# Prepared weights in groups of 1024 columns, four words apart, in a two-model transformer kernel

## The reference, cut to what matters

```python
for l in range(2):                                     # first block
    h = rmsnorm(x, norm_mix[l]); proj = h @ w_in[l]    # q, k, v, u, ug, ga, gb
    merged = sigmoid(ga) * attention(q, k, v) + sigmoid(gb) * (conv(u, ug) @ w_conv_out[l])
    x = x + merged @ w_out[l]
    g, up = split(rmsnorm(x, norm_ffn[l]) @ w_gate_up[l])
    x = x + (silu(g) * up) @ w_down[l]                 # w_down: 2816 x 1024
proj = rmsnorm(x, g_pre_mix_2) @ w_in_2                # second block
y_ret = retention(q, k, v, g) @ w_ret_o_2
y_sgu = (gelu(u) * spatial(layernorm(gelu(sv)))) @ w_sgu_o_2
x = x + rmsnorm((sigmoid(a_ret) * y_ret + sigmoid(a_sgu) * y_sgu) @ w_out_2, g_post_mix_2)
x = x + rmsnorm(conv_gated_mlp(rmsnorm(x, g_pre_ffn_2), w_up_2, w_down_2), g_post_ffn_2)
```

## Time and profile before

| what | value |
|---|---|
| median of the 2 runs | 2197.49 us (2197.23 to 2197.76) |
| span of the profiled execution | 2195.6 us |
| TensorE busy (10,528 matmuls) | 2182.7 us, 99% |
| weight loads busy | 1813.8 us, 83% |
| VectorE busy | 1378.5 us, 63% |
| ScalarE busy | 965.5 us, 44% |
| GpSimd busy | 74.7 us, 3% |
| DMA | 208.39 MB, 95 GB/s, 27% of the 16 engines' time |

### The profile page before, as it was taken

How to read it: one execution, slowest core, us unless ns; L and a number is a source line. 1 busy time by engine, 2 the same in 40 slices (tenths; PEclk the granted TensorE clock), 3 DMA queues, 4 the chain that set the end, 5 groups by cost and what they waited for, 6 DMA issues and landing times.

```text
span 2195.6 us, 28930 instructions
## 1 busy us (share of the span) xinstructions
PE 2182.7 (99%) x10528; PEld 1813.8 (83%) x10528; DVE 1378.5 (63%) x1978; ACT 965.5 (44%) x1392; POOL 74.7 (3%) x103
## 2 busy tenths in 40 slices
PE   9999999999999999999999999999999999999998
PEld 6878888888888878888888888888888899888887
DVE  7999954444345999954444334654776568888723
ACT  5678544443223588544443223331554344333412
POOL 0000020000010000020000010000000000000000
PEclk9999999999999999999999999999999999999999
DMA  5221222222223211222222224223222231222222
GB/s 182 75 78 65 96 96 96 96 96 84 93 93 123 90 62 64 94 96 100 99 99 92 80 92 156 97 77 131 84 91 87 96 135 39 100 101 97 94 96 77
DMA packets 35397, 208.39 MB, mean 95 GB/s; under 512 B 4512, under 2 KB 5024, under 8 KB 14816
## 3 DMA queue, kind: packets, MB, share of 16 engines
q1 hardware_dynamic: 35296, 207.07, 27.0%
HBM read 201.15 MB, written 2.10 MB: 93 GB/s over the span
## 4 chain that ended last, share of the span: by engine, by line
PE 94%; ACT 3%; DVE 2%; issue 1%; DMA 0%; SPq 0%; DVEq 0%
PE mm L1794 25%; PE mm L1796 25%; PE mm L1795 25%; PE sp L1794 4%; PE sp L1795 4%; PE sp L1796 4%; PE sp L1896 1%; PE ob L1924 1%; DVE conv_y L1171 1%; ACT probs L584 1%; DVE probs L1201 1%; ACT probs L592 1%; PE sp L1911 0%; DMA x<-in_x_dram 0%; PE ob L1796 0%
## 5 line engine op out<-in xcount | busy, mean ns | idle before, releaser
L1794 PE MATMUL mm<-in_hi,w_hi 128*128 128x512 f32 (+1 forms) x1696 | 663.8, 391 | 3.8 <-DVE in_lo L1104 2.1
L1796 PE MATMUL mm<-in_hi,w_lo 128*128 128x512 f32 (+1 forms) x1696 | 657.0, 387 | 0.0
L1795 PE MATMUL mm<-in_lo,w_hi 128*128 128x512 f32 (+1 forms) x1696 | 657.0, 387 | 0.0
L525 ACT ACTIVATE w_hi<-w_raw 128x2048 fp32r<-128x2048 f32 (+3 forms) x193 | 346.2, 1794 | 674.8 <-PE mm L1796 557.9
L1070 DVE TENSOR_TENSOR w_lo<-w_raw,w_hi 128x2048 fp32r<-128x2048 f32 (+3 forms) x193 | 422.3, 2189 | 239.5 <-ACT w_hi L525 239.0
L1794 PEld LDWEIGHTS mm<-in_hi,w_hi 128*128 128x128 f32 x1696 | 318.5, 188 | 75.1 <-DVE in_lo L1104 6.0
L1796 PEld LDWEIGHTS mm<-in_hi,w_lo 128*128 128x128 f32 x1696 | 318.4, 188 | 65.8
L1795 PEld LDWEIGHTS mm<-in_lo,w_hi 128*128 128x128 f32 x1696 | 318.6, 188 | 64.1 <-issue 1.0
L1171 DVE SCALAR_TENSOR_TENSOR conv_y<-conv_in,parl,conv_y 128x512 f32<-128x512 f32 x240 | 170.0, 747 | 1.7
L1081 DVE TENSOR_TENSOR tB<-mm,rstd 128x512 f32<-128x512 f32 x54 | 37.3, 691 | 172.8 <-PE mm L1796 172.8
L1794 PE MATMUL mm<-act_hi,w_hi 128*128 128x512 f32 x352 | 136.9, 389 | 0.0
(11 more groups left out here) (429 smaller groups left out, 3257.0 us busy)
## 6 DMA issues: line engine op xcount, KB each, us to landing
w_raw<-in_w_dram SPq DMA_DIRECT2D x160, 1024.0 KB, 4.8
w_raw<-in_w_dram SPq DMA_DIRECT2D x32, 704.0 KB, 3.9
w_raw<-in_w_dram SPq DMA_DIRECT2D x5, 512.0 KB, 4.7
out_dram<-z_rows SPq DMA_DIRECT2D x8, 256.0 KB, 2.1
rope<-in_rope_dram SPq DMA_DIRECT2D x3, 512.0 KB, 3.6
x<-in_x_dram SPq DMA_DIRECT2D x4, 256.0 KB, 4.9
x<-in_x_dram SPq DMA_DIRECT2D x2, 512.0 KB, 7.9
sq<-ssum SPq DMA_DIRECT2D x32, 32.0 KB, 1.8
```

The lines of the kernel that those rows point to most:

```text
L525: e.activation(whi[:, slot, 0:cols], raw[:, slot, 0:cols], ACT.Copy).then_inc(s_whi, whi_out.up())
L1794: MM(out, ah, bh, start=first, stop=False, **kw)
L1795: MM(out, ah, bl, start=False, stop=False, **kw)
L1796: return MM(out, al, bh, start=False, stop=last, **kw)
```

## The change

The slots of w_hi and w_lo become two groups of 1028 columns, of which 1024 are used: the tensors are [128, 2, 2, 1028] in place of [128, 2, 2048]. From the tensor's start, the tiles of slot 0 group 0 begin at multiples of 512 bytes as before, those of slot 0 group 1, slot 1 group 0 and slot 1 group 1 at 16, 32 and 48 bytes past one. Each tensor is 64 bytes longer. The unused tensor to_512_bytes goes. w_raw and the loads stay as they are.

Helpers turn a column range into a place. A range of more than 1024 columns always becomes both groups whole, 2048 columns; so down's preparation of 1408 columns, on ScalarE and on VectorE, now works on 2048, of which the last 640 hold what an earlier chunk left.

```diff
+GROUP = CH // 2 + 4
...
-        whi = sb("w_hi", [P, 2, CH], F32R)
-        wlo = sb("w_lo", [P, 2, CH], F32R)
+        whi = sb("w_hi", [P, 2, 2, GROUP], F32R)
+        wlo = sb("w_lo", [P, 2, 2, GROUP], F32R)
...
-        sb("to_512_bytes", [P, 92])
...
+        def w_cols(t, slot, a, b):
+
+            h = CH // 2
+            if b - a > h:
+                return t[:, slot, 0:2, 0:h]
+            return t[:, slot, a // h, a % h:a % h + b - a]
+
+        def w_tile(t, slot, k):
+
+            return t[:, slot, k // KT, k % KT * P:k % KT * P + P]
+
+        def raw_cols(slot, a, b):
+
+            if b - a > CH // 2:
+                return raw[:, slot, :].rearrange("p (k c) -> p k c", k=2)
+            return raw[:, slot, a:b]
...
-                e.activation(whi[:, slot, 0:cols], raw[:, slot, 0:cols], ACT.Copy).then_inc(s_whi, whi_out.up())
+                e.activation(w_cols(whi, slot, 0, cols), raw_cols(slot, 0, cols), ACT.Copy).then_inc(s_whi, whi_out.up())
...
-                TT(wlo[:, slot, first:cols], raw[:, slot, first:cols], r32(whi[:, slot, first:cols]),
+                TT(w_cols(wlo, slot, first, cols), raw_cols(slot, first, cols), r32(w_cols(whi, slot, first, cols)),
                    ALU.subtract).then_inc(s_w, w_out.up())
...
-                    a = slice((at + j) * P, (at + j + 1) * P)
-                    ins = mm3(four[bank], whi[:, slot, a], wlo[:, slot, a], hi_[:, k, :], lo_[:, k, :],
+                    ins = mm3(four[bank], w_tile(whi, slot, at + j), w_tile(wlo, slot, at + j), hi_[:, k, :], lo_[:, k, :],
                               first and j == 0, last and j == len(ks) - 1)
...
-                    ws = slice(j * D + d * T, j * D + d * T + T)
+                    ws = (c % 2, j * D + d * T, j * D + d * T + T)
...
-                    ins = mm3(rows[b][d], acth[:, k, ts], actl[:, k, ts], whi[:, c % 2, ws], wlo[:, c % 2, ws],
+                    ins = mm3(rows[b][d], acth[:, k, ts], actl[:, k, ts], w_cols(whi, *ws), w_cols(wlo, *ws),
                               k == 0, k == FT - 1)
```

More of the change, by code:

```diff
@@ L533, in prep_part @@
             def prep_part(cs):
-                e.activation(whi[:, 0, cs], raw[:, 0, cs], ACT.Copy).then_inc(s_whi, whi_out.up())
+                e.activation(w_cols(whi, 0, cs.start, cs.stop), raw_cols(0, cs.start, cs.stop), ACT.Copy).then_inc(s_whi, whi_out.up())
             def prep_rest():
@@ L1115, in prep_and_sum @@
                 for cs in (slice(0, CH // 2), slice(CH // 2, CH)):
-                    TT(wlo[:, 1, cs], raw[:, 1, cs], r32(whi[:, 1, cs]), ALU.subtract).then_inc(s_w, w_out.up())
+                    TT(w_cols(wlo, 1, cs.start, cs.stop), raw_cols(1, cs.start, cs.stop),
+                       r32(w_cols(whi, 1, cs.start, cs.stop)), ALU.subtract).then_inc(s_w, w_out.up())
                     if cs.start == 0:
@@ L1136, in _ @@
             first_lo((2,))
-            more = slice(CH // 4, CH // 2)
             e.wait_ge(s_whi, whi_in.next())
-            TT(wlo[:, 0, more], raw[:, 0, more], r32(whi[:, 0, more]), ALU.subtract).then_inc(s_do, own.up())
+            TT(w_cols(wlo, 0, CH // 4, CH // 2), raw_cols(0, CH // 4, CH // 2), r32(w_cols(whi, 0, CH // 4, CH // 2)),
+               ALU.subtract).then_inc(s_do, own.up())
             first_lo((3,))
@@ L2011, in token_major @@
                         e.wait_ge(ready.sem, ready.next())
-                    ws = slice(256 * k, 256 * k + 256)
-                    ins = mm3(mm[bank][:, 0:256], xh[:, k, ts], xl[:, k, ts], whi[:, slot, ws], wlo[:, slot, ws],
+                    ws = (slot, 256 * k, 256 * k + 256)
+                    ins = mm3(mm[bank][:, 0:256], xh[:, k, ts], xl[:, k, ts], w_cols(whi, *ws), w_cols(wlo, *ws),
                               k == 0, k == KT - 1)
@@ L2025, in wide @@
                         e.wait_ge(ready.sem, ready.next())
-                    ws = slice(T * j, T * j + T)
-                    ins = mm3(four[wide_banks[b]], xh[:, k, ts], xl[:, k, ts], whi[:, slot, ws], wlo[:, slot, ws],
+                    ws = (slot, T * j, T * j + T)
+                    ins = mm3(four[wide_banks[b]], xh[:, k, ts], xl[:, k, ts], w_cols(whi, *ws), w_cols(wlo, *ws),
                               k == 0, k == KT - 1)
@@ L2122, in half_product @@
                         e.wait_ge(ready.sem, ready.next())
-                    a = slice(at + k * P, at + (k + 1) * P)
-                    ins = mm3(out, wh[:, a], wl[:, a], xh[:, k, hs], xl[:, k, hs], k == 0, k == KT - 1)
+                    a = slice(k * P, (k + 1) * P)
+                    ins = mm3(out, wh[:, at, a], wl[:, at, a], xh[:, k, hs], xl[:, k, hs], k == 0, k == KT - 1)
                 return ins
@@ L2136, in out_half @@
             def out_half(m, hs, ks=range(KT), ready=None):
-                return half_product(four[m % 4][:, 0:TH], wo[:, m // 2, 0, :], wo[:, m // 2, 1, :],
-                                    CH // 2 * (m % 2), hs, ready, ks)
+                wh, wl = (wo[:, m // 2, i, :].rearrange("p (k c) -> p k c", k=2) for i in range(2))
+                return half_product(four[m % 4][:, 0:TH], wh, wl, m % 2, hs, ready, ks)
             def up_half(j, hs, ks=range(KT), ready=None):
-                return half_product(four[j][:, hs], whi[:, j // 2, :], wlo[:, j // 2, :],
-                                    CH // 2 * (j % 2), hs, ready, ks)
+                return half_product(four[j][:, hs], whi[:, j // 2, :, :], wlo[:, j // 2, :, :],
+                                    j % 2, hs, ready, ks)
             e.wait_ge(s_w, w_in.next())
@@ L2192, in _ @@
                         e.wait_ge(s_mmf, taken.next())
-                        half_product(bank, whi[:, c, :], wlo[:, c, :], CH // 2 * d,
+                        half_product(bank, whi[:, c, :, :], wlo[:, c, :, :], d,
                                      slice(0, T)).then_inc(s_mm, tiles.up())
```

## The result

| kernel | median us (lowest to highest) | runs | span of the profiled execution |
|---|---|---|---|
| before | 2197.49 (2197.23 to 2197.76) | 2 | 2195.6 |
| changed | 2235.17 (2234.96 to 2235.38) | 2 | 2233.1 |

The changed kernel takes 1.0172 times the time of before, with a 95% interval of 1.0156 to 1.0189: +37.7 us, where +17.6 was forecast. The time moved the way that was forecast but a little over twice as far, to where rival C had put it (2231 to 2240).

A forecast was written before the change was run, and what follows sets the result against it. TensorE's pace was taken to bound the kernel. Terms of 9.3 and 8.3 us, the others 0, gave +17.6 us: 2213 on the profiled span, 2215 us by the median; own range 2198 to 2231, stated range 2180 to 2264.

The forecast's parts named there:

- rival C: All products: groups change faster than the rhythm settles, or settling needs phase 0; +33 to +43 us, 2231 to 2240; chance 0.14.
- What bounds the kernel: Whole kernel: TensorE busy 2182.7 of 2195.6 us at full clock; only its pace or a new wait can change the time.
- Part 1: Stationary weight tiles: each of 344 changes of group disturbs the rhythm for 27 ns, +9.3 us; bounds 0 to 18 us.
- Part 2: Weights as streamed operand (wide, token_major, rows_product): 828 shifted matmuls at 10 ns, +8.3 us; bounds 0 and 11.
- Part 3: Pad gone, weight tensors 64 bytes longer, so w_lo, x and in_hi move: taken at 0, bound 10 ns a product.
- rival D: Toll: every product with a shifted operand pays 10 ns wherever that operand sits; +66 us, 2263 us; chance 0.13.
- Part 4: Preparation, down's 1,408 columns rounded up to 2,048 on ScalarE and VectorE: covered, taken at 0; +4 us if slack is overdrawn.
- the 15.0 forecast: Down loop: sign that the prediction is right, its 66 matmuls taking 15.0 us.
- A (relief): Shifted products escape a 13.3 ns collision of weight load and stream: -88 us, 2110, chance 0.11; mild form 2180, chance 0.03.
- B (nothing felt): TensorE is indifferent to 16-byte offsets; the sums' 399 ns come from waits ahead of sum_halves; 2197 us; chance 0.15.
- a mean of 394 everywhere (C): Matmul durations in the trace: a sign that the prediction is wrong and the rhythm never settles.

The follow-up runs named there:

- the map: Four variants of the changed kernel, the groups' weight tiles at other phases (64 to 192, 80 to 112, 144 to 176, -48 to -16 bytes): 2229.05, 2244.62, 2233.95, 2224.73 us.
- the sums' move: The kernel before with parl and pars allocated behind the small tensors, so sum_lo, square_lo and sq begin at the common phase: 2196.94 us, ratio 0.9999.

## Why the prediction was wrong, step by step

**What bounds the kernel** held: the time moved with TensorE's pace alone, at a full clock, with no new wait.

**Part 1, stationary tiles: the step that failed.** The prediction put it: "Within a group (8 tiles, 24 matmuls) the phase is constant; each change of group is a shift", and charged 344 shifts with 27 ns each, on the belief that constant phase means 226.7 ns. The runs show that the settled distance is itself a function of the phase between stationary tile and stream: 226.7 ns at 0, 233.3 at 32 and 48 bytes in the kernel with only the steps, and those are paid by every matmul. The 27 ns themselves are right, but they are paid only on the return to phase 0, one change in four. With the steps alone, parts 1 and 2 together are worth +27.2 us, not +17.6; by the distances 26.6 us fall to the products of part 1, which was put at 9.3. The evidence was read too narrowly: the earlier trace rows show how the rhythm comes back to 226.7 **at phase 0**, the only phase at which any long stretch of before runs. They can't say what it settles to elsewhere. The earlier trace rows had a hint, 399 ns at 32 bytes, which a single matmul could not tell from a disturbance; and the earlier trace rows, plain fp32 at about 100 ns with two columns, were no evidence on loads that run beside a 213 ns stream.

**Part 3, the 64 bytes of w_lo, taken at 0** with the remark that no row shows such a phase: +32.5 us alone. This was the bigger error in size. The bound, rival D's 10 ns a product, was the right place for it, but it was carried as a rival with a chance of 0.13 instead of as a term of the sum between 0 and 10 ns a product; the middle of that, 5 ns on 8,544, is 43 us. The growth of w_lo looked like a side effect of the change, and yet it moves an operand of every third matmul.

**The parts don't add.** 27.2 + 32.5 = 59.7 against 37.7 measured, since both set the same quantity: with w_lo 64 bytes off every group already runs at 231.1, and with the steps on top the four lie between 231 and 233.3.

**Part 2, streamed weights, +8.3 us**: too dear, and no term of its own. In the last stage the streamed weights are at 393 to 395, the level of everything else, and the 256-column ones of token_major fell by 2 ns a start. The distances give +3.4 us for the streamed weights of 512 columns and -1.1 us for everything of 256. What matters is the difference of the two addresses, not which of the two operands moved.

**Part 4, preparation: right.** ScalarE in down, timeline of the changed kernel, against the earlier trace rows:

```profile
581.26 1.92 ACT L542 ACTIVATE w_hi<-w_raw 128x2048 fp32r<-128x2048 f32 x1 [5.72 <-PE mm L1814]
596.55 1.93 ACT L542 ACTIVATE w_hi<-w_raw 128x2048 fp32r<-128x2048 f32 x1 [5.72 <-PE mm L1814]
```

1.92 in place of 1.38 us, still waiting 5.72 us for PE. The 66 matmuls take 15.29 us, 231.7 ns each, not the 15.0 forecast; that is part 1's error again. VectorE's subtraction is 2.29 and, disturbed, 3.39 us; no product in down waits for it:

```profile
600.29 3.39 DVE L1087 TENSOR_TENSOR w_lo<-w_raw,w_hi 128x2048 fp32r<-128x2048 f32 x1
606.15 2.29 DVE L1087 TENSOR_TENSOR w_lo<-w_raw,w_hi 128x2048 fp32r<-128x2048 f32 x1 [2.48 <-ACT w_hi L542]
```

The kernel with in_hi alone moved, at before's time with this preparation, shows the 0.

**The rivals.** A (relief) fell for 512 columns at every phase tried; its one true part is token_major. Warm back-to-back matmuls at 215.7 ns, as the Trainium skill has them (TensorE: Matmul & The Clock Gate, "Wait — 56ns, not 53.3ns?"), were not reached at any phase: the trace does not agree with it for these f32r products, whose lowest is 226.7. B (nothing felt) fell to the map and to the sums' move. C (never settles, 5 ns each, 2231 to 2240) is what happened, in the second of its two forms, "its settled state needs phase 0" (with the steps alone, two of four groups do settle at 226.7). Its price was right, 231.8 - 226.95 = 4.9 ns over 8,478 matmuls, though it came from disturbances that only happen to cost the same on average. D was too dear, and its mechanism, a toll on the operand, is refuted by weights and streams moved together. The prediction's own test, "a mean of 394 everywhere (C)", decided it at first sight. The fault was the chance of 0.14: the case for settling again rested on two stretches at one phase.

**Open.** What in TensorE or in its reads makes the distance depend on phase was not found. The Trainium skill, TensorE: Matmul & The Clock Gate, "Step-by-step: what each phase is for", says that loading the next tile's weights takes no read bandwidth from the running matmul. The pair with weights and streams both at +32 (226.7) and streams alone at +32 (233.3) speaks against reading that as independence of the two: where each reads from sets the pace. Whether they meet in a bank, a row or a line, no run here tells. Nor is it the pair read at one time alone that counts: with w_lo alone off by 64 bytes, its tile is loaded beside line 1825's stream, and the distance there is 229 ns; the 236 come one matmul later, beside the load of a w_hi tile at phase 0.

## What to carry to other kernels

Where weight load and stream alternate back to back, treat the start addresses of **all** operands as one set: in this kernel all congruent modulo 256 bytes was the fastest layout tried for 512 columns, and one tensor grown by 64 bytes (w_lo, in every third matmul) cost 1.5%. Before resizing or removing a tensor, list what is allocated behind it, and read the distance between starts for each operand pair, since 389 against 394 ns of duration is the whole effect. And a constant measured where a kernel always is (a settled pace, a recovery) says nothing of a state it never enters: price that state as an interval and put the interval into the sum.

## What the runs showed that was not expected

- **256 bytes from phase 0 it is as at phase 0, and nowhere between is it better.** With the prediction's 213.3 ns for the stream itself, an estimate: 226.7 = 213.3 + 13.3 ns at phase 0; 231.9 to 234.3 at most others, 233.3 = 213.3 + 20 the commonest; 228.9 and 229.7 at 192 and 176. That other phases repeat after 256 bytes was not run.
- **Its sign turns with the width.** 256 columns run at 120.0 = 106.7 + 13.3 ns at phase 0 and down to 113.3, 106.7 + 6.7, with the streamed weights 112 bytes on.
- **Two stable paces at one phase.** At 16 bytes both 226.7 and 233.3 are held for hundreds of matmuls, and two waits of 0.1 to 0.2 us changed the lower into the higher. At phase 0 the lower one always comes back.
- **Where the stretch of a cycle falls.** With w_lo alone off by 64 bytes the cycle is 228, 229, 236 ns: of the 13 ns that three matmuls lose against 3 x 226.7, 9.3 stand behind one of them.
